# Sampled dilated attention moved out of a block of its own and woven into the compression; later modulation moved into the prompt attention

## The chip, the cores and the metric

The kernel runs on one core of one Trainium2 chip. The metric is device time in microseconds (us) of one execution. A core has five engines with queues of their own: TensorE (PE; its weight loads are shown as PEld), VectorE (DVE), ScalarE (ACT), GpSimd (POOL) and SyncE (SP, which here only issues transfers). They work in parallel and wait for one another on semaphores. Transfers are issued from the queues of SP, ACT and POOL and run on 16 DMA engines.

## The reference

One layer of a hybrid decoder, for a prompt of 512 tokens and for 8 sampled sequences of 4 tokens each (32 sampled tokens), with the same weights. Cut to what the change touches:

```
mod = silu(c) @ w_ada + b_ada                      # six groups of 1024: shift, scale, gate of mixer and of FFN
sh_m, sc_m, g_m, sh_f, sc_f, g_f = split(mod, 6)

# compression (branch A): rows of the key and value cache, paged, 4096 past tokens per sampled sequence
kc = compress_rows(kvc_full[:, 0], w1, pe, w2)     # conv of length 32, stride 16; gelu; @ w2
vc = compress_rows(kvc_full[:, 1], ...)

# dilated attention (branch C): 3 groups of 4 heads, (window, dilation) = (128,1), (512,4), (2048,16)
krow = n_prefix + q0 + arange(qb)[:, None] - offs[None, :]      # 129 rows of the cache for each query
s = einsum('bqhd,bhqkd->bhqk', q, kvg[:, 0]) * dk**-0.5 - bias
p, lse = masked_softmax(s, krow >= 0)
o = einsum('bhqk,bhqkd->bqhd', p, kvg[:, 1])
o_c = einsum('gbth,gbthd->bthd', softmax(lses), outs)           # the 3 groups merged
```

The first two of the six modulation groups are needed at once; the other four only after the mixer.

## The kernel before

The program is a chain of blocks. In each, every engine runs its own list of instructions in the order in which the code writes them, and the next block starts when all engines have ended theirs. Around the change the blocks are, in order:

1. `project_and_mix` (L1209): projection and the recurrent mixer. Several generators are merged on each engine by `weave` (L292): each yields a number, its place, and the generator with the lowest place writes its instructions next. The order is thus fixed when the program is built.
2. `sample_dilated` (L2433): the dilated attention of the 32 sampled tokens. One partition is one (head, sequence, token), 128 in all. For each of the three groups and for keys, then values, 129 rows of 64 numbers per partition are loaded into one of three buffers (`kv0` to `kv2`, 4.2 MB each), DVE multiplies a whole buffer by the query (L2569) and reduces it (L2570), ACT takes the exponential (L2523), and DVE multiplies the values by the weights (L2577) and reduces (L2578). Keys are loaded from SP's queue and values from POOL's (L2477 to L2485). In groups 1 and 2 the rows lie apart, so a transfer is made of pieces of 256 bytes; 16 large transfers make a buffer, each to 8 partitions. ACT's queue loads the four later modulation groups (`w_ada`, 16 MB in 8 transfers, L2518), PE multiplies them (L239, `modulation_step`), turns them (L246), and DVE adds the bias (L253). At its end SP issues 81 small transfers that write the new rows of the caches (`new_cache_rows`, L514).
3. `compress` (L1243): 36 units of work w, (sequence s, part c): 9 sequences (8 sampled, then the prompt) by 4 (keys and values of two heads). POOL gathers the pages of one whole sequence with 8 indirect transfers of 0.5 MB (L1307) into one of two buffers of four parts. For each unit PE transposes (L1337, `turn`), DVE splits each result into a high and a low part (L274, L279, `keep`), PE makes 48 matmuls (L1355, `hidden`), ACT applies gelu (L1389), PE projects (L1366, L1370), DVE copies the result. `turn(w + 1)` stands before `hidden(w)`.
4. `prompt_attention` (L1744): 48 units, 32 of kind A (8 heads, 4 query blocks; block qt sees qt + 1 blocks of keys) and 16 of kind C. PE: scores, transposes, values; DVE: bias and maximum; ACT: exponential, evacuation; POOL: scaling. SP loads the inputs, waits for them, and issues four large copies of the old caches to the outputs (`shift_caches`, L549, 47 MB).
5. `sample_nsa` and the rest, which the change leaves alone.

A `Chain` (L82) makes an engine wait for each of its own instructions before the next.

## Time and profile before

| | us |
|---|---|
| median of 3 runs | 2797.47 (2796.63 to 2809.92) |
| the profiled execution | 2810.91 |
| its span, first to last instruction | 2809.1 |
| PE busy | 2036.8 (73%) |
| DVE busy | 1357.4 (48%) |
| ACT busy | 442.3 (16%) |
| POOL busy | 310.0 (11%) |
| mean granted TensorE clock | 0.832 |

A span is cut into blocks by the first instruction of each. Busy times of engines overlap. The granted clock is a share of 2.4 GHz: 0.5 stands for 1.2 GHz, 1.0 for 2.4 GHz, and a value between says that a stretch held both. The DMA share is the mean busy share of the 16 DMA engines; since the packets of several queues overlap on an engine it can read a little over 1. A duration on SPq is how long SP was held by issuing the transfer, not how long the data took.

### The profile page before, as it was taken

How to read it: one execution, taken by the hardware profiler on the slowest of the kernel's cores; microseconds unless marked ns; L12 is line 12 of the kernel's file. 1: busy time of each engine (PE TensorE's matmuls, PEld its weight loads, DVE VectorE, ACT ScalarE, POOL GpSimd, SP SyncE). 2: the span in 40 equal slices, each digit the busy share in tenths (PEclk: the TensorE clock that was granted, in tenths of full speed). 3: DMA queues.
4: the chain of work that ended last, by engine and by line, in shares of the span. 5: the costliest groups of instructions: out<-in, count | busy, mean ns of one | idle time of the engine just before them, and what ended most of it. 6: DMA issues, size and time to landing. Idle time of an engine off the chain costs nothing. (4 is left out here: it accounts for less than half of the span.)

```text
span 2809.1 us, 38178 instructions
## 1 busy us (share of the span) xinstructions
PE 2036.8 (73%) x16050; PEld 1729.2 (62%) x16050; DVE 1357.4 (48%) x2126; ACT 442.3 (16%) x976; POOL 310.0 (11%) x350
## 2 busy tenths in 40 slices
PE   4986889789921002999959988127777976999995
PEld 2985778788910002899956566013435856999994
DVE  2135666665305533666605665454572346444444
ACT  1242333222200000000004454001111000000000
POOL 0000000000021212122003454004120000000000
PEclk7997999999965555999955898558878997999997
DMA  7434313122466863333139900127245103233220
GB/s 233 126 103 121 84 44 81 47 71 79 122 217 168 163 127 115 117 128 127 37 128 326 313 33 1 36 64 269 95 147 214 48 1 87 87 91 89 80 66 32
DMA packets 291913, 317.20 MB, mean 113 GB/s; under 512 B 92573, under 2 KB 246934, under 8 KB 287135
## 3 DMA queue, kind: packets, MB, share of 16 engines
q1 hardware_dynamic: 263998, 215.82, 26.2%
q0 software_dynamic: 24320, 79.94, 9.1%
q10 hardware_dynamic: 3424, 19.01, 2.1%
q8 instruction: 128, 2.10, 0.3%
q14 instruction: 43, 0.34, 0.0%
HBM read 287.10 MB, written 79.71 MB: 131 GB/s over the span
## 5 line engine op out<-in xcount | busy, mean ns | idle before, releaser
L307 PE MATMUL inp_acc<-hh,inp_wh 128*128 128x272 f32 (+1 forms) x1072 | 342.9, 320 | 32.6 <-DVE inp_wl L279 18.6
L307 PE MATMUL inp_acc<-hh,inp_wl 128*128 128x272 f32 (+1 forms) x1072 | 316.6, 295 | 0.0
L307 PE MATMUL inp_acc<-hl,inp_wh 128*128 128x272 f32 (+1 forms) x1072 | 316.2, 295 | 0.0
L307 PEld LDWEIGHTS inp_acc<-hh,inp_wh 128*128 128x128 f32 (+1 forms) x1072 | 207.9, 194 | 55.0 <-issue 27.7
L279 DVE TENSOR_TENSOR inp_wl<-inp_w,inp_wh 128x1024 fp32r<-128x1024 f32 (+1 forms) x67 | 81.2, 1213 | 268.4 <-ACT inp_wh L459 267.9
L307 PEld LDWEIGHTS inp_acc<-hl,inp_wh 128*128 128x128 f32 (+1 forms) x1072 | 208.5, 195 | 3.5 <-issue 3.1
L307 PEld LDWEIGHTS inp_acc<-hh,inp_wl 128*128 128x128 f32 (+1 forms) x1072 | 207.7, 194 | 0.5
L288 PE MATMUL ffn_acc<-ffn_hh,ffn_wh 128*128 128x272 f32 x704 | 147.3, 291 | 36.4 <-DVE ffn_wl L279 36.4
L1355 PE MATMUL cmp_pH<-cmp_RTh,cmp_w1h 128*128 128x256 f32 (+1 forms) x576 | 171.1, 297 | 2.7 <-issue 2.7
L1355 PE MATMUL cmp_pH<-cmp_RTh,cmp_w1l 128*128 128x256 f32 (+1 forms) x576 | 167.7, 291 | 3.0 <-issue 3.0
L1355 PE MATMUL cmp_pH<-cmp_RTl,cmp_w1h 128*128 128x256 f32 (+1 forms) x576 | 168.1, 292 | 2.0 <-issue 2.0
L1896 POOL TENSOR_SCALAR pat_s<-pat_s,pat_st 128x31 f32<-128x31 f32 (+2 forms) x144 | 127.3, 902 | 287.2 <-DVE pat_st L1924 238.8
L288 PE MATMUL ffn_acc<-ffn_hl,ffn_wh 128*128 128x272 f32 x704 | 146.6, 290 | 0.0
L288 PE MATMUL ffn_acc<-ffn_hh,ffn_wl 128*128 128x272 f32 x704 | 145.1, 287 | 0.0
L239 PE MATMUL sdi_acc<-sdi_w,cT 128*32 128x512 f32 x128 | 26.7, 979 | 153.2 <-DMA sdi_w<-in_w_ada_dram 153.2
L288 PEld LDWEIGHTS ffn_acc<-ffn_hh,ffn_wh 128*128 128x128 f32 x704 | 110.9, 190 | 36.8 <-DVE ffn_wl L279 36.8
L1355 PEld LDWEIGHTS cmp_pH<-cmp_RTl,cmp_w1h 128*128 128x128 f32 x576 | 118.2, 205 | 3.4 <-issue 3.4
L1355 PEld LDWEIGHTS cmp_pH<-cmp_RTh,cmp_w1h 128*128 128x128 f32 x576 | 117.6, 204 | 3.5 <-issue 3.1
L1355 PEld LDWEIGHTS cmp_pH<-cmp_RTh,cmp_w1l 128*128 128x128 f32 x576 | 117.5, 204 | 2.2 <-issue 2.2
L288 PEld LDWEIGHTS ffn_acc<-ffn_hl,ffn_wh 128*128 128x128 f32 x704 | 111.8, 190 | 0.0
L239 PEld LDWEIGHTS sdi_acc<-sdi_w,cT 128*32 128x32 f32 x128 | 4.6, 152 | 174.0 <-DMA sdi_w<-in_w_ada_dram 163.8
L288 PEld LDWEIGHTS ffn_acc<-ffn_hh,ffn_wl 128*128 128x128 f32 x704 | 111.5, 190 | 0.0
(443 smaller groups left out, 4109.1 us busy)
## 6 DMA issues: line engine op xcount, KB each, us to landing
inp_w<-in_w_in_dram SPq DMA_DIRECT2D x66, 512.0 KB, 4.3
out_dram<-in_cache_dil_dram SPq DMA_DIRECT2D x1, 32704.0 KB, 152.7
ffn_w<-in_w_ffn_dram SPq DMA_DIRECT2D x60, 512.0 KB, 4.0
sdi_w<-in_w_ada_dram ACTq DMA_DIRECT2D x8, 2048.0 KB
PT<-inp_o SPq DMA_DIRECT2D x58, 272.0 KB
sdi_kv<-in_cache_dil_dram POOLq DMA_DIRECT2D x36, 256.0 KB, 12.2
sdi_kv<-in_cache_dil_dram SPq DMA_DIRECT2D x36, 256.0 KB
ada_wada<-in_w_ada_dram SPq DMA_DIRECT2D x8, 1024.0 KB, 9.3
```

Of the source, the lines that this page charges most:

```text
L239: i = pe.matmul(out[32 * j:32 * j + 32, :], cT[:, k, :], w[:, 512 * j:512 * j + 512], start=(k == 0), stop=(k == KD - 1))
L279: return eng.tensor_tensor(lo, x, hi.bitcast(F32), ALU.subtract)
L288: i = pe.matmul(out[:, h, 0:HN], l, r[:, h * HN:(h + 1) * HN], start=(first and n == 0), stop=(last and n == 2))
L307: i = pe.matmul(out, l, r, start=(first and n == 0), stop=(last and n == 2))
L1355: i = pe.matmul(pH[:, w % 2, 0:nw], l, r, start=(q == 0 and n == 0), stop=(q == 15 and n == 2))
L1896: pool.tensor_scalar(s[:, u % 3, b, 0:n], s[:, u % 3, b, 0:n], st[:, u % 4, 2, b:b + 1], None, ALU.mult).then_inc(sd, 1)
```

## The change

`sample_dilated` is gone as a block. Its attention becomes the class `Dilated` (L1482 of the changed kernel), the compression becomes `Compression` (L1243), and `compress_and_dilate` (L1639) weaves the two in one block. The three buffers of 129 rows become three of 43 rows, so there are 18 loads ("pieces") instead of 6, all from SP's queue. The high part in the compression is written by ACT instead of DVE. The gathers go into a ring of six units instead of two sequences; the prompt's unit is read from `TM` by POOL's queue. The loads and matmuls of the later modulation are put between the units of the prompt attention, and `shift_caches` is issued from ACT's queue there. The wait for the new rows moves to the end of the program.

```
+class Compression:
+    NR = 6
+        self.R = lambda w: first[:, w % 6] if w % 6 < 4 else second[:, w % 6 - 4]
+    def pool(self, pool):
+        for w, (s, c) in enumerate(self.work):
+            if w >= self.NR:
+                pool.wait_ge(self.turned, self.read(w - self.NR))
+            elif w == 4:
+                pool.wait_ge(self.wfree, 3)
+            if s < DB:
+                for h in range(2):
+                    pool.indirect_dma_start(...).then_inc(self.got[w % self.NR], 16)
+    def tensor(self, pe):
+        for w in range(len(self.work)):
+            yield w
+            if w + 1 < len(self.work):
+                turn(w + 1)
+            yield w + 0.2
+            hidden(w)
+            yield w + 0.9
+            if w:
+                project(w - 1)
+    def scalar(self, act):
+                yield w + 0.1
+                high(w + 1)          # activation(RTh, pT, Copy), 4 per unit
+            yield w + 0.85           # then gelu of unit w
+    def vector(self, dve):
+                for j, x in enumerate(self.keep_at(w + 1)):
+                    yield w + 0.12 + 0.1 * j
+                    low(*x)          # split_low only
+            if w:
+                yield w + 0.95
+                result(w - 1)
+class Dilated:
+    NK = 129
+    PIECE = 43
+    NB = 3
+        self.order = keys[0] + keys[1] + vals[0] + keys[2] + vals[1] + vals[2]   # 3 pieces each
+    def transfers(self, i):
+        g, v, p = self.order[i]
+        return 16 if p < 2 else 32 if g == 0 else 20
+    def sync(self, sp):
+        self.load(sp, 0)
+        sp.wait_ge(self.qk, 2)
+        sp.dma_start(a["QC"], self.qt[:, :]).then_inc(self.qst, 16)
+        sp.wait_ge(self.qst, 16)
+        ...                          # 4 loads of the queries from QC
+        for i in range(1, len(self.order)):
+            if i >= self.NB:
+                sp.wait_ge(self.used, i - self.NB + 1)
+            self.load(sp, i)
+        new_cache_rows(sp, a, m["token_rows_out"])
+    def at(self, i, k):
+        return 0.5 + 1.8 * i + k
+    def vector(self, dve):
+        for i, (g, v, p) in enumerate(self.order):
+            yield self.at(i, 0)
+            if i == 0:
+                dve.wait_ge(self.loaded, 16 * 5)
+            dve.wait_ge(self.here[i % self.NB], self.arrived(i))
+            if v == 0:
+                c(dve.tensor_tensor(x, x, q..., ALU.mult))
+                yield self.at(i, 0.9)
+                c(dve.tensor_reduce(s[:, g, r], x, AX, ALU.add))
+                dve.sem_inc(self.used, 1)
+            ...                      # values alike
+        yield 50
+        dve.wait_ge(self.ft, 1)      # PE's last transpose; then 4 copies to ocT
 def prompt_attention(nc, a, m):
+    mod_at = [3 + 2 * l for l in range(KD)] + [24 + 2 * l for l in range(KD)]
+    turn_at = [mod_at[KD - 1] + 3, mod_at[2 * KD - 1] + 3]
-                sp.wait_ge(loaded, NLOAD)
-                shift_caches(sp, a, m["copied"])
+                for l in range(2 * KD):
+                    if l >= 4:
+                        sp.wait_ge(mstep, l - 3)
+                    sp.dma_start(wada[:, l % 4, :], a["w_ada"][...]).then_inc(wl[l % 4], 16)   # 1 MB
+                    if i in mod_at:                       # PE
+                        pe.wait_ge(wl[l % 4], 16 * (l // 4 + 1))
+                        modulation_step(pe, pM[:, :], m["cT"], wada[:, l % 4, :], l % KD).then_inc(mstep, 1)
+                    if i in turn_at:                      # PE
+                        pe.wait_ge(mevac, n + 1)
+                        modulation_turn(pe, pM[:, :], mm[:, n], m["ident"]).then_inc(mturned, 1)
                 act.wait_ge(loaded, NLOAD)
+                shift_caches(act, a, m["copied"])
-            sample_dilated(nc, a, m)
-NSA = [compress, prompt_attention, sample_nsa]
+NSA = [compress_and_dilate, prompt_attention, sample_nsa]
```

How the order moves on DVE, in the compression at the units around the first value pieces. Before, in the compression, the two halves of a split stood in a row, with nothing of the dilated branch:

```order
L274 CAST cmp_RTh<-cmp_pT 128x4x128
L279 TENSOR_TENSOR cmp_RTl<-cmp_pT,cmp_RTh 128x4x128
L274 CAST cmp_RTh<-cmp_pT 128x4x128
L279 TENSOR_TENSOR cmp_RTl<-cmp_pT,cmp_RTh 128x4x128
L274 CAST cmp_RTh<-cmp_pT 128x4x128
L279 TENSOR_TENSOR cmp_RTl<-cmp_pT,cmp_RTh 128x4x128
```

And the changed kernel, same engine (sdi_kv is a piece of 43 rows, cmp_RTl the low part that PE waits for, sdi_o the reduced values):

```order
L279 TENSOR_TENSOR cmp_RTl<-cmp_pT,cmp_RTh 128x4x128 x2
L1615 TENSOR_TENSOR sdi_kv<-sdi_kv,sdi_s 128x2752
L279 TENSOR_TENSOR cmp_RTl<-cmp_pT,cmp_RTh 128x4x128 x2
L1464 COPY vc<-cmp_pK 128x64
L1464 COPY vc<-cmp_pK 127x64
L279 TENSOR_TENSOR cmp_RTl<-cmp_pT,cmp_RTh 128x4x128
L1617 TENSOR_REDUCE sdi_o<-sdi_kv 128x64
L279 TENSOR_TENSOR cmp_RTl<-cmp_pT,cmp_RTh 128x4x128 x3
```

The casts have left DVE, and one instruction of a piece stands between the low parts of nearly every unit; the multiplication waits for the piece's transfers, and the low parts behind it wait with it.

On SP, the stretch from the last large loads to the new rows. Before:

```order
L2477 DMA sdi_kv<-TM 32x64
L2485 DMA sdi_kv<-in_cache_dil_dram 8x128x64 x4
L2477 DMA sdi_kv<-TM 32x64
L2485 DMA sdi_kv<-in_cache_dil_dram 8x128x64 x4
L519 DMA out_dram<-TM 512x4x64 x3
L525 DMA out_dram<-TM 128x4x64 x2
```

In the changed kernel:

```order
L1540 DMA sdi_kv<-in_cache_dil_dram 8x43x64 x32
L1529 DMA sdi_kv<-TM 32x64
L1540 DMA sdi_kv<-in_cache_dil_dram 8x42x64 x4
L1529 DMA sdi_kv<-TM 32x64
L1540 DMA sdi_kv<-in_cache_dil_dram 8x42x64 x4
L1529 DMA sdi_kv<-TM 32x64
L1540 DMA sdi_kv<-in_cache_dil_dram 8x42x64 x4
L1529 DMA sdi_kv<-TM 32x64
L1540 DMA sdi_kv<-in_cache_dil_dram 8x42x64 x4
L519 DMA out_dram<-TM 512x4x64 x3
```

The new rows keep their place behind the last load, but that load now waits for DVE's work on an earlier piece, late in the compression, and the loads that POOL issued stand on SP as well.

On PE, the prompt attention from its third unit on (pat_pS scores, pat_pX transposes, pat_pO values). Before:

```order
L1823 MATMUL pat_pS<-pat_kA,pat_qA 128x128 x2
L1835 MATMUL pat_pX<-ident,pat_s 31x128
L1835 MATMUL pat_pX<-ident,pat_s 128x128 x2
L1823 MATMUL pat_pS<-kcT,pat_qA 128x31
L1823 MATMUL pat_pS<-pat_kA,pat_qA 128x128 x2
```

In the changed kernel:

```order
L2051 MATMUL pat_pS<-pat_kA,pat_qA 128x128 x2
L2063 MATMUL pat_pX<-ident,pat_s 31x128
L2063 MATMUL pat_pX<-ident,pat_s 128x128 x2
L239 MATMUL pat_pM<-pat_wada,cT 32x512 x4
L2051 MATMUL pat_pS<-kcT,pat_qA 128x31
L2051 MATMUL pat_pS<-pat_kA,pat_qA 128x128 x2
```

One modulation step of four matmuls stands ahead of every second unit's scores, sixteen times in all.

## Rows read from the trace of the kernel before

**Rows 1.** Timeline: first SP issue of each block; start us, us, engine, line.

```profile
787.96 0.37 SPq L2492 DMA_DIRECT2D sdi_qf<-PT  x1
...
1087.98 0.37 SPq L1286 DMA_DIRECT2D cmp_pt<-in_page_lanes_dram  x1
...
1445.88 1.31 SPq L1798 DMA_DIRECT2D pat_qA<-PT  x2
...
1757.46 1.28 SPq L1992 DMA_DIRECT2D sco_qd<-PT  x2
```

**Rows 2.** Windows: span, busy us (count) of PE, PEld, DVE, ACT, POOL, clock, DMA share, GB/s.

```profile
1137.00:1400.00 263.00, 254.07 (x2075) 243.29 (x2073) 170.23 (x288) 16.18 (x33) 45.09 (x48) 0.99 0.29 99
...
1476.00:1545.00 69.00, 63.61 (x218) 43.74 (x219) 35.65 (x152) 27.21 (x122) 23.18 (x39) 0.50 1.02 332
1545.00:1757.00 212.00, 188.88 (x971) 128.77 (x970) 124.72 (x393) 95.47 (x328) 104.16 (x105) 0.88 0.36 115
```

**Rows 3.** Tile sdi_kv: DVE's passes over a whole buffer; duration ns min/median/max.

```profile
L2569 DVE TENSOR_TENSOR sdi_kv<-sdi_kv,sdi_q x3: 8758/8759/8760, 860.0 to 1025.3; 128x8256 f32<-128x8256 f32 x3
L2570 DVE TENSOR_REDUCE sdi_s<-sdi_kv x3: 8753/8753/8754, 868.8 to 1034.1; 128x129 f32<-128x8256 f32 x3
...
L2578 DVE TENSOR_REDUCE sdi_o<-sdi_kv x3: 13918/14032/14036, 887.7 to 1053.0; 128x64 f32<-128x8256 f32 x3
```

**Rows 4.** Groups by line: the split in the compression, DVE; busy us, mean ns.

```profile
L279 DVE TENSOR_TENSOR cmp_RTl<-cmp_pT,cmp_RTh 128x512 fp32r<-128x512 f32 (+1 forms) x136 | 90.8, 668 | 4.7
L274 DVE CAST cmp_RTh<-cmp_pT 128x512 fp32r<-128x512 f32 (+1 forms) x136 | 89.7, 660 | 19.8 <-PE cmp_pT L1337 19.7
```

**Rows 5.** Source line 467: ACT copying 128x512 out of PSUM, ns min/median/max.

```profile
L467 ACT ACTIVATE inp_tok<-inp_tb x18: 575/599/601, 174.5 to 407.1; 128x512 f32<-128x512 f32 x18
```

**Rows 6.** Timeline: PE at the compression's start, then ACT's gelu of three units.

```profile
1121.31 5.24 PE L1337 MATMUL cmp_pT<-ident,cmp_R 128*128 128x128 f32 x24 [6.57 <-DMA cmp_R<-in_cache_nsa_cmp_dram,idx]
...
1130.73 0.56 PE L1355 MATMUL cmp_pH<-cmp_RTh,cmp_w1h 128*128 128x256 f32 x1
...
1145.25 0.47 ACT L1389 ACTIVATE cmp_hid<-cmp_pH,cmp_hc 128x255 f32<-128x255 f32 x1 [5.63 <-PE cmp_pH L1355]
1153.44 0.47 ACT L1389 ACTIVATE cmp_hid<-cmp_pH,cmp_hc 128x255 f32<-128x255 f32 x1 [7.72 <-PE cmp_pH L1355]
...
1399.78 0.47 ACT L1389 ACTIVATE cmp_hid<-cmp_pH,cmp_hc 128x255 f32<-128x255 f32 x1 [6.61 <-PE cmp_pH L1355]
```

**Rows 7.** Windows, columns as rows 2: SP alone loading, SP and POOL loading, gathers.

```profile
860.00:880.00 20.00, 0.00 (x0) 0.00 (x0) 19.19 (x5) 0.50 (x2) 1.67 (x3) 0.50 0.52 112
...
920.00:940.00 20.00, 0.00 (x0) 0.00 (x0) 2.27 (x1) 0.00 (x0) 2.13 (x2) 0.50 0.90 123
...
1120.00:1130.00 10.00, 5.93 (x29) 5.44 (x29) 5.53 (x9) 0.00 (x0) 4.59 (x5) 0.67 1.03 413
```

**Rows 8.** Tile sdi_kv, SP's issues of group 0: ns min/median/max.

```profile
L2481 SPq DMA_DIRECT2D sdi_kv<-in_cache_dil_dram x16: 629/666/3230, 789.0 to 817.9; - x16
```

**Rows 9.** Timeline of SP: four loads among bulk transfers; the new rows, first and last.

```profile
877.36 33.49 SPq L2485 DMA_DIRECT2D sdi_kv<-in_cache_dil_dram  x4
...
1020.40 6.69 SPq L519 DMA_DIRECT2D out_dram<-TM  x3
...
1082.67 3.86 SPq L540 DMA_DIRECT2D out_dram<-TM  x6
```

**Rows 10.** Waits of PE from 1137 to 1400: us in total, times, longest.

```profile
PE cmp_pH L1355 <- issue: 7.7, 11, 1.1
```

**Rows 11.** Timeline: PE's modulation steps (8 records each); SP issuing the cache copies.

```profile
810.10 1.92 PE L239 MATMUL sdi_acc<-sdi_w,cT 128*32 128x512 f32 x16 [0.75 <-DMA sdi_w<-in_w_ada_dram]
...
904.00 3.64 PE L239 MATMUL sdi_acc<-sdi_w,cT 128*32 128x512 f32 x16 [7.39 <-DMA sdi_w<-in_w_ada_dram]
...
1471.66 0.64 SPq L556 DMA_DIRECT2D out_dram<-in_cache_nsa_win_dram  x1
1472.35 1.88 SPq L556 DMA_DIRECT2D out_dram<-in_cache_dil_dram  x3
```

More of the change, by code:

```diff
@@ new lines, in keep_at, with high @@
+    def keep_at(self, w):
+        s, c = self.work[w]
+        for k in range(self.mark[w], self.read(w)):
+            h, kq = (k - self.mark[w]) // 2, (k - self.mark[w]) % 2
+            yield (k, (slice(None), w % 2, slice(kq * 4, kq * 4 + 4), slice(h * P, h * P + self.rows(s))),
+                   self.pT[:, k % 4, :].rearrange("p (j c) -> p j c", j=4)[:, :, 0:self.rows(s)])
+    def scalar(self, act):
+        nc = self.nc
+        def high(w):
+            if w >= 2:
+                act.wait_ge(self.hd, w - 1)
+            for k, at, x in self.keep_at(w):
+                act.wait_ge(self.turned, k + 1)
+                nc.scalar.activation(self.RTh[at], x, ACT.Copy).then_inc(self.high, 1)
+        yield -0.9
+        act.wait_ge(self.wfree, 2)
+        high(0)
+        for w, (s, c) in enumerate(self.work):
+            if w + 1 < len(self.work):
+                yield w + 0.1
+                high(w + 1)
+            yield w + 0.85
+            act.wait_ge(self.hd, w + 1)
+            if w >= 2:
+                act.wait_ge(self.od, w - 1)
+            if w == 0:
+                act.wait_ge(self.hck, 1)
+            nc.scalar.activation(self.hid[:, w % 2, 0:self.nwin(s)], self.pH[:, w % 2, 0:self.nwin(s)], ACT.Gelu_apprx_tanh,
+                                 bias=self.hc[:, c // 2:c // 2 + 1]).then_inc(self.act, 1)
@@ L1300, in _ @@
[L1300 to L1310 removed]
+                cmp.pool(pool)
@@ L1312, in _ @@
             @block.tensor
             def _(pe):
-                pe.wait_ge(loaded, 80)
-                pe.transpose(pK[:, 0, 0:32], per[:, :], m["ident"][0:32, 0:32]).then_inc(pet, 1)
-                pe.wait_ge(pek, 1)
-                for v in range(2):
-                    for c in range(16):
-                        i = pe.matmul(pH[:, 0, v:v + 1], w1[:, v, c, :], peT[:, v * 16 + c:v * 16 + c + 1], start=(c == 0), stop=(c == 15))
-                i.then_inc(hcd, 1)
-                pe.wait_ge(hck, 1)
@@ L1342, in hidden @@
-                def hidden(w):
-                    s, c = work[w]
-                    pe.wait_ge(tkept, tmark[w] + 2 * nhalf(s))
-                    if w >= 2:
-                        pe.wait_ge(act_, w - 1)
-                    nw = nwin(s) + 1
-                    if w == 0:
-                        pe.wait_ge(wfree, 3)
-                    for q in range(16):
-                        lo, hi = w1l[:, c // 2, q, :], w1h[:, c // 2, q, :]
-                        x = slice(q // 8, q // 8 + nw)
-                        xh, xl = RTh[:, w % 2, q % 8, x], RTl[:, w % 2, q % 8, x]
-                        for n, (l, r) in enumerate(((hi, xh), (hi, xl), (lo, xh))):
-                            i = pe.matmul(pH[:, w % 2, 0:nw], l, r, start=(q == 0 and n == 0), stop=(q == 15 and n == 2))
-                    i.then_inc(hd, 1)
@@ L1444, in _ @@
-                keep(0)
-                for w in range(len(work)):
-                    if w + 1 < len(work):
-                        keep(w + 1)
-                    if w:
-                        result(w - 1)
-                result(len(work) - 1)
+                weave(cmp.vector(dve), dil.vector(dve))
 def layer_norm_t(nc, a, m, tag, xin, out_tokens=None, gain="ln1"):
```

588 lines of the change are left out of this document (295 added, 293 removed).

## The prediction, made blind

> **What bounds the kernel now.** I read the timeline of SP first, for where one block ends and the next begins [rows 1]. The dilated branch holds the core from 787.96 to 1087.98 us, 300.0 us; the compression from there to 1445.88, 357.9 us; the prompt attention to 1757.46, 311.6 us. Then the windows, for who is busy in each. In the steady compression PE is busy 254 of 263 us at the full clock, DVE 170, ACT 16, and the DMA share is 0.29 [rows 2]: PE sets the end, and DVE, ACT and the DMA engines have room. Which room, the tiles tell. A pass of DVE over a whole buffer takes 8.76 us (the weighting of the values has the same shape) and the reduction of the values 14.03 [rows 3], so three groups cost 3 x (8.76 + 8.75 + 8.76 + 14.03) = 120.9 us of DVE. In the attention PE is busy 63.6 of 69 us at half clock up to 1545, and 188.9 of 212 us at a mean of 0.88 afterwards [rows 2]: PE bounds it too, closely at first and less so later.
>
> **Part 1, the block removed.** All of 300.0 us goes: DVE, DMA waits, and the new rows that SP issues last [rows 1]. This is the one large gain. What it held must now fit beside the compression (dilated attention, new rows) and beside the attention (modulation).
>
> **Part 2, DVE and ACT in the compression.** A unit takes PE 1153.44 - 1145.25 = 8.2 us in steady state, and (1399.78 - 1145.25)/30 = 8.5 us on average over the 30 units from w = 1 to 31 [rows 6]; I use 8.5. The four casts of a unit (0.66 us each) leave DVE, which keeps four subtractions (0.67 us) [rows 4], 2.7 us, and about 0.4 us of results. A piece is a third of a buffer: 2.9 + 2.9 us for keys, 2.9 + 4.7 us for values [rows 3], one piece every 1.8 units, so 3.2 to 4.2 us per unit. DVE then has 6.3 to 7.3 us of work in 8.5. ACT gets four copies of 128x512 out of PSUM at 0.6 us [rows 5], with gelu 2.9 us per unit. Neither becomes the bound. A low part can now be late by one DVE instruction, 4.7 us at most; `turn(w + 1)` precedes the 48 matmuls of unit w, most of its 8.2 us, so the four subtractions still end within the unit. I cost this at nothing; if the cover is gone it is 1 to 2 us in a few units.
>
> **Part 3, the transfers of the pieces, where I see the new bound.** A piece is 128 x 43 x 256 bytes = 1.41 MB. In groups 1 and 2 (12 of 18 pieces) it moves in 256-byte parts. SP alone moved these at 112 GB/s with a DMA share of 0.52; SP and POOL together at 123 GB/s with a share of 0.90 [rows 7]. So a second queue brought nothing, and a piece takes 11.5 to 12.6 us; I take 12. Its 16 issues (0.67 us each [rows 8], 10.7 us) lie within that; the last piece of three has 20, I take 15 us, and 32 in group 0, 21 us. Gathers ran at 413 GB/s [rows 7]: 1.05 MB per unit is 2.5 us, 4.6 us in 1.8 units. Do the two add up or overlap? The nearest row says that added traffic is paid: four loads of 1 MB in all held SP for 33.5 us while bulk transfers ran [rows 9], 9 us by the rate alone. I take the sum, 17 us for a piece with gathers beside it, against 1.8 x 8.5 = 15.3 us in which PE uses one up. The bounds are 12.5 (full overlap) and 20.
>
> The Trainium skill ("DMA: Bandwidth & Descriptors", section "Why a DMA increments its semaphore by 16 and not by 1") states that a transfer is spread over the largest number up to 16 that divides its slowest dimension, on SP's queue over the lowest-numbered engines. These transfers go to 8 partitions, so by that rule all pieces would sit on the same 8 engines, which agrees with the share of 0.52; gathers on all 16 would queue behind them there, and the sum (17) would hold rather than the overlap (12.5).
>
> Now SP's chain, in us from the block's start. The queries come back from `QC` near 37, when SP can go on to piece 1. Pieces 1 and 2 (11 and 21) end at 69. Pieces 3, 4, 5: 17 + 17 + 19, at 122. Pieces 6 to 8 (group 0's values, large parts): 12 + 12 + 21, at 167. Pieces 9 to 14: 106, at 273. Gathers, six units ahead, are over by then: 12 + 12 + 15, at 312. Behind it stand the 81 new rows, which took 1086.5 - 1020.4 = 66 us [rows 9]: SP ends at 378. PE's chain: the first hidden matmul came 42.7 us after the block's start, after a wait of 6.6 us for gathers of a whole sequence [rows 6]; two gathers are enough now, I take 39 (bounds 36 and 43). Piece i is needed at 39 + 8.5 x (0.5 + 1.8 i): 89 for piece 3, 120 for 5, 201 for 10, 257 for 14. By the chain above they land at about 88, 124, 203 and 275: PE loses some 17 us behind DVE's wait in all. Then 357.9 - 42.7 - 1 = 314 us of units as before, and 2 us for the last transpose and copies: 39 + 314 + 17 + 2 = 372. SP ends later, 378, plus the 1.5 us from its last issue to the next block as before: **379.5 us against 357.9, +21.6**. Bounds: with full overlap SP is held back only by the buffers (piece 14 consumed near 267, + 15 + 66 = 348) and PE ends at 355, so -1; with 20 us for each of the nine pieces beside gathers, +49. Instruction fetches stopped PE 11 times for 7.7 us [rows 10] at a DMA share of 0.29; with more traffic I expect more, within the 6 us by which PE trails SP.
>
> **Part 4, the attention.** The input loads are unchanged. The four cache copies, 0.64 + 1.88 us of issue on SP [rows 11], now stand ahead of ACT's first scaling, on which PE waits: +2.5. A modulation step takes 3.64/2 = 1.8 us at half clock and 1.92/2 = 0.96 at full [rows 11]. Of the 16, six fall into the half-clock stretch: 6 x 1.8 + 10 x 0.96 = 20.5 us. PE has hardly a gap for them. The two turns, with waits for ACT and DVE, 3. Against that, the step is dense, and after two in a row the clock rose even in idle surroundings, while the attention's first 69 us ran at 0.50 [rows 2]. If the steps lift it there for a third of the time, about 10 us come back (bounds 0 and 30, half of 63.6). Sum 2.5 + 20.5 + 3 - 10 = **+16**, between -4 and +26. The w_ada loads (1 MB per two units, 10 us or so) share the engines with 47 MB of copies at 332 GB/s [rows 2]; four buffers of lead cover that.
>
> **Sum.** 2809.1 - 300.0 + 21.6 + 16 = 2546.7 us of span, 2548.5 with the 1.8 us around it. The profiled execution (2810.9) is 13.4 us above the median of three, one of which is as long. Taking that off: **2535 us**.
>
> **Rivals.**
> A, the transfers overlap: part 3 gives -1 instead of +21.6 and part 4 +5, as the clock rises more: 2535 - 23 - 11 = 2501. For it: a share of 0.52 leaves half the engine time free. Against: rows 9.
> B, the transfers add up more badly: 20 us per piece (+27) and no help from the clock (+10): 2572. For it: the 33.5 us. Against: those bulk loads were far denser than the gathers.
> C, PE loses its instructions: if each of the 36 units had a stop of 2.4 us instead of 7.7 us in all, 86 - 8 = 78 more, less the 6 of slack: 2607. Against: the present stops are 1.1 us at most [rows 10], though at gather bursts.
> D, slower than before: every piece is starved as in the 33.5 us row. 1 MB in 33.5 us makes 45 us per piece, 17 of them 765, with 37 before and 66 + 1.5 after: 869.5, +512 instead of +22, so 3025. It decides from (357.9 + 284 - 104.5)/17 = 31.6 us per piece. It needs bulk traffic all the time, while gathers alone need 2.5 us of 8.5.
> E, the weaving brings nothing beyond moving the wait (PE stops for each piece and its clock halves): a unit then costs up to double at half clock; at a third of the 31 large units, 10 x 8 = 80, 2615. The share of PE's waiting would have to be far above the 17 us worked out.
>
> **Chances.** Forecast 0.44, A 0.26, B 0.18, C 0.04, E 0.04, D 0.03, 0.01 for a time below A. Predicted 2535. The range runs from 2490, a little below A, to 2600, B with its execution in the upper of the two levels seen; it leaves out C, D, E and the tails. A measurement of this kernel can tell some 0.5% (14 us) from no change. Faster 0.95, same 0.02, slower 0.03.
>
> **What would show it.** Block lengths from SP's first issues: the compression 360 to 400 us; under 360 says A. Its end: last issue of the new rows, not PE's last transpose; the other way round says that SP is not the bound. DVE's wait for sdi_kv: near zero for pieces 0 to 4, then 2 to 5 us at heavy pieces. SP held about 17 us per heavy piece. DVE busy near 75% there. In the attention 16 steps, half of them near 1.8 us and a clock above 0.5 before the 384-column scores. Wrong would be: DVE or ACT as the last releaser of PE's transposes without a piece behind it, a wait of PE for w_ada, or a compression above 410 us.

## The result, and the profile of the changed kernel

The changed kernel takes 2641.27 us (median of 4 runs, 2634.51 to 2647.57), the kernel before 2803.27 us beside it (2796.63 to 2809.92). The ratio is 0.942, 95% interval 0.939 to 0.945: 5.8% faster. The prediction was 2535 us, range 2490 to 2600. Its direction was right; it was 106 us too fast, and the time lies outside its range.

Its profiled execution took 2641.51 us, with a span of 2639.7. The timeline of SP gives the block starts again (start, us, engine, line), to be laid beside [rows 1]:

```profile
790.46 0.33 SPq L1285 DMA_DIRECT2D cmp_pt<-in_page_lanes_dram  x1
...
1189.45 1.36 SPq L2022 DMA_DIRECT2D pat_qA<-PT  x2
...
1589.69 1.25 SPq L2242 DMA_DIRECT2D sco_qd<-PT  x2
```

| us | before | forecast | after |
|---|---|---|---|
| up to the compression (dilated block included before) | 1088.0 | 788.0 | 790.5 |
| compression | 357.9 | 379.5 | 399.0 |
| prompt attention | 311.6 | 327.6 | 400.2 |
| the rest | 1051.6 | 1051.6 | 1050.0 |

So the block that went gave 297.5 us where 300 were forecast (with the blocks ahead of it, which the change leaves alone, ending 2.5 us later), the compression took 19.5 us more than forecast, and the attention 72.6 us more. The attention is the larger miss, so I read it first. Windows of the changed kernel (span, busy us and count of PE, PEld, DVE, ACT, POOL, clock, DMA share, GB/s), a stretch of the compression and two of the attention:

```profile
833.00:1110.00 277.00, 243.13 (x1930) 233.27 (x1930) 190.02 (x195) 84.40 (x157) 61.86 (x52) 0.94 0.65 178
...
1230.00:1340.00 110.00, 63.11 (x237) 36.58 (x238) 30.00 (x127) 22.13 (x105) 20.92 (x36) 0.53 1.01 341
1340.00:1500.00 160.00, 129.38 (x695) 79.47 (x694) 77.59 (x259) 60.54 (x212) 64.02 (x69) 0.85 0.38 131
```

PE is busy 63 of 110 us where [rows 2] had 63.6 of 69, and its clock stays at 0.53. The DMA engines are full (1.01, 341 GB/s). The waits of the attention's stretch (us in total, times, longest) and the timeline of PE's modulation steps name what it stands behind:

```profile
PE pat_pM L239 <- DMA pat_wada<-in_w_ada_dram: 67.3, 5, 19.9
```

```profile
1252.13 1.93 PE L239 MATMUL pat_pM<-pat_wada,cT 128*32 128x512 f32 x8
...
1270.33 1.94 PE L239 MATMUL pat_pM<-pat_wada,cT 128*32 128x512 f32 x8 [7.39 <-DMA pat_wada<-in_w_ada_dram]
...
1302.08 1.94 PE L239 MATMUL pat_pM<-pat_wada,cT 128*32 128x512 f32 x8 [19.52 <-DMA pat_wada<-in_w_ada_dram]
...
1333.38 1.94 PE L239 MATMUL pat_pM<-pat_wada,cT 128*32 128x512 f32 x8 [19.87 <-DMA pat_wada<-in_w_ada_dram]
...
1364.60 1.94 PE L239 MATMUL pat_pM<-pat_wada,cT 128*32 128x512 f32 x8 [19.78 <-DMA pat_wada<-in_w_ada_dram]
```

The first four loads were issued ahead of the copies. The first three are in time, the fourth comes 7.4 us late (the row at 1270.33); then a megabyte comes every 31 us (1302.08, 1333.38, 1364.60), while two units of PE's work take 10 to 12. The page's section on transfers (KB each, median us from issue to landing; packets and MB of ACT's queue):

```profile
out_dram<-in_cache_dil_dram ACTq DMA_DIRECT2D x1, 32704.0 KB, 161.8
pat_wada<-in_w_ada_dram SPq DMA_DIRECT2D x16, 1024.0 KB, 27.8
...
q10 hardware_dynamic: 2080, 50.23, 5.5%
```

In the compression the waits of its stretch, then SP's timeline and DVE's last work in the block:

```profile
DVE sdi_kv L1605 <- DMA sdi_kv<-in_cache_dil_dram: 52.1, 6, 11.7
PE cmp_pT L1332 <- DVE cmp_RTl L279: 33.8, 8, 7.7
...
DVE sdi_kv L1615 <- DMA sdi_kv<-in_cache_dil_dram: 13.6, 6, 6.3
```

```profile
860.01 37.76 SPq L1540 DMA_DIRECT2D sdi_kv<-in_cache_dil_dram  x32
...
1121.57 5.63 SPq L519 DMA_DIRECT2D out_dram<-TM  x3
...
1183.65 3.86 SPq L540 DMA_DIRECT2D out_dram<-TM  x6
```

```profile
1174.86 0.77 DVE L1636 COPY ocT<-cmp_pK 64x32 f32<-64x32 f32 x4 [0.58 <-PE cmp_pK L1576]
```

DVE waited 65.7 us for pieces, and PE 33.8 us behind it, where the forecast had PE lose 17. SP ends last, as forecast: 12 us after DVE's last copy (1187.5 against 1175.6) where the forecast had 6, and both later than forecast.

### The profile page after: what moved, and what is told of

Read it like the earlier page. It is cut to its first block and busy times, and to the rows that moved or that the text cites. A ratio compares the mean times of both kernels' runs of the same rounds, so it can differ in the third digit from the quotient of the medians.

```text
span 2639.7 us, 38466 instructions
## 1 busy us (share of the span) xinstructions
PE 2032.3 (77%) x16050; PEld 1728.5 (65%) x16050; DVE 1271.1 (48%) x2016; ACT 520.9 (20%) x1119; POOL 270.6 (10%) x282
## 3 DMA queue, kind: packets, MB, share of 16 engines
q10 hardware_dynamic: 2080, 50.23, 5.5%
## 5 line engine op out<-in xcount | busy, mean ns | idle before, releaser
L307 PE MATMUL inp_acc<-hh,inp_wh 128*128 128x272 f32 (+1 forms) x1072 | 342.7, 320 | 32.7 <-DVE inp_wl L279 18.5
L1306 POOL DMA_INDIRECT cmp_R<-in_cache_nsa_cmp_dram,idx x44 | 51.1, 1162 | 860.7 <-DVEq L1433 748.4
L2113 ACT ACTIVATE pat_s<-pat_s,pat_st 128x31 f32<-128x31 f32 (+2 forms) x144 | 70.2, 488 | 228.6 <-DVE pat_st L2155 173.5
## 6 DMA issues: line engine op xcount, KB each, us to landing
pat_wada<-in_w_ada_dram SPq DMA_DIRECT2D x16, 1024.0 KB, 27.8
```

The lines of the kernel that those rows point to most:

```text
L307: i = pe.matmul(out, l, r, start=(first and n == 0), stop=(last and n == 2))
L1306: pool.indirect_dma_start(out=self.R(w)[:, h, :], out_offset=None, in_=src, in_offset=bass.IndirectOffsetOnAxis(ap=self.m["idx"][:, c, 2 * ...
L2113: nc.scalar.activation(s[:, i % 3, b, 0:n], s[:, i % 3, b, 0:n], ACT.Exp, bias=st[:, i % 4, 0, b:b + 1], accum_out=st[:, i % 4, 1, b:b + 1 ...
```

## Experiments

The theories at the start. **W**: the `w_ada` loads are starved by the cache copies. **P**: the sixteen steps cost that much by themselves. For the compression, **G**: pieces and gathers add up on the transfers; against it, that DVE's and ACT's new work delays PE. The chip varies between sessions: the kernel before took 2810 to 2811 us (medians) beside runs 1 to 8 and 2779 to 2780 beside 9 to 12, where the blocks behind the attention take 13 us less. I therefore compare by ratio to the kernel before, and by blocks. No trace of the kernel before was taken beside runs 9 to 12, so where the other 18 of its 31 us went isn't known; the ratios of these runs are the surer measure. The blocks are those of one profiled execution each. Where a run leaves transfers out or splits them, the counts that are waited for change with it and aren't shown.

| run | compression | attention | rest | ratio |
|---|---|---|---|---|
| changed kernel | 399.0 | 400.2 | 1050.0 | 0.942 (0.939 to 0.945) |
| 1 copies late | 397.5 | 316.9 | 1111.6 | 0.933 (0.930 to 0.936) |
| 2 no loads | 394.4 | 336.6 | 1050.1 | 0.917 (0.913 to 0.920) |
| 3 finer cut | 398.6 | 407.2 | 1051.6 | 0.940 (0.935 to 0.944) |
| 4 rows moved | 383.5 | 439.8 | 1053.4 | 0.949 (0.946 to 0.953) |
| 5 packets 19 KB | 394.8 | 373.2 | 1050.6 | 0.927 (0.922 to 0.932) |
| 6 packets 5 KB | 398.7 | 369.2 | 1047.7 | 0.927 (0.923 to 0.931) |
| 7 no gathers | 347.1 | 410.6 | 1051.4 | 0.923 (0.918 to 0.929) |
| 8 no pieces | 341.5 | 406.6 | 1050.1 | 0.920 (0.914 to 0.926) |
| 9 paced | 398.4 | 328.7 | 1037.1 | 0.918 (0.915 to 0.921) |
| 10 paced, early piece | 397.1 | 327.1 | 1037.1 | 0.916 (0.912 to 0.919) |
| 11 all | 381.5 | 315.8 | 1036.5 | 0.913 (0.911 to 0.915) |
| 12 half rows | 393.3 | 436.0 | 1037.5 | 0.956 (0.953 to 0.960) |

### 1. The copies issued late

```
                 for l in range(2 * KD):
                     ...                       # wait, load of w_ada
+                sp.wait_ge(mstep, 2 * KD)
+                shift_caches(sp, a, m["copied"])
-                shift_caches(act, a, m["copied"])
```

> The changed kernel, with the four cache copies (47 MB) issued by SP after the last modulation step instead of by ACT at the start of the prompt attention. Theory W (the 1 MB loads of w_ada are starved by the copies, PE stands behind each, and its clock stays low): no wait of PE for w_ada (67 us in the changed kernel), and the attention falls from 400 us to 311.6 + 16 - 2.5 = 325 us. The copies then run for some 160 us, most of it in the next block: the rest grows by 0 to 30 us. In all 2641 - 75 + (0 to 30) = 2566 to 2596 us. Rival P (the sixteen steps of matmuls cost this much by themselves, by their own time at half clock and by what they push back): the attention stays above 380 us, all in all 2620 to 2641. Rival C (whoever runs beside the copies pays the same price as the modulation did): the attention falls by 75 us and the rest grows by as much, 2641.

The attention fell to 316.9 us, below what W expected, with no wait of PE for `w_ada`; a load landed 4.9 us after its issue (median) instead of 27.8. Theory P is out. But 62 of the 83 us came back in the next block, more than W allowed and near to rival C. The waits from the next block on, and the windows of the attention's first 80 us and of the next block's:

```profile
DVE sna_QD L2308 <- DMA sco_tri<-in_c_tri_dram: 98.7, 1, 98.7
```

```profile
1223.00:1303.00 80.00, 77.98 (x335) 44.82 (x334) 41.41 (x167) 30.13 (x135) 28.12 (x45) 0.66 0.31 104
...
1503.00:1583.00 80.00, 0.00 (x0) 0.00 (x0) 0.00 (x0) 0.00 (x0) 0.00 (x0) 0.50 0.87 276
```

The next block begins with loads too, and they were late in the same way: that wait was 35.7 us in the changed kernel. Here too the bulk copy delayed who loaded beside it. In the attention the steps, now on time, cost 316.9 - 311.6 = 5.3 us net. The clock is at 0.66 in the window from 40 to 120 us after the block's start, where the same stretch of the kernel before (1486 to 1566 us) has 0.61; how much of the steps' price that gave back, the run doesn't tell.

### 2. The loads left out

```
+                    if l < 4:
                         sp.dma_start(wada[:, l % 4, :], ...)
-                        pe.wait_ge(wl[l % 4], 16 * (l // 4 + 1))
+                        pe.wait_ge(wl[l % 4], 16)
```

> The changed kernel without the w_ada loads 5 to 16 (left out; the steps multiply the first four buffers again), with the cache copies where they were. It tells the price of the steps beside the copies from that of the late loads. Theory W: PE waits for nothing here once the first four loads are in, the attention takes 325 to 335 us, in all about 2570. Rival P: the steps themselves cost, the attention stays near 400, 2640. Rival I (the copies slow PE in another way, through its instruction fetches): PE's idle time without a releaser is tens of us and the attention stays above 370 us.

336.6 us with the copies where they were and all sixteen steps on PE: W, 1.6 us above its range. Rival I is out, since PE has no wait without a releaser in the block. One of the first four loads still came 8.5 us late. What is left over before is 336.6 - 311.6 = 25.0 = 8.5 + 2.7 (ACT's issues) + 13.8 for steps and turns, net of what the clock gave; the forecast had 20.5 + 3 - 10 = 13.5.

### 3. The copies cut finer

```
-... ("dil1", 512, 8, 4), ("dil2", 2048, 8, 28)):
+... ("dil1", 512, 8, 16), ("dil2", 2048, 8, 112)):
```

> The changed kernel with the two largest cache copies cut four times finer (pieces of 4.7 KB instead of 18.7 KB for the largest); bytes, queue and place as before. Theory T (a DMA engine takes a piece from each queue in turn, so a queue's share goes by the size of its pieces): w_ada's rows of 8 KB got 1 MB in 30 us, about 35 GB/s of 330; against pieces a quarter as large its share at least doubles, a load takes 8 to 15 us, and the attention falls to 330 to 350 us; in all 2570 to 2590. Rival B (the share doesn't hang on the pieces' size, the loads stand behind bytes already queued): a load stays at 30 us and the attention at 400, 2641. A cost of the finer pieces themselves would show as a longer time of the copies than 162 us.

PE waited 67.4 us for `w_ada`, and it is no evidence for rival B: ACT's queue held the same packets as before, so the finer cut never reached the queue: neighbouring pieces that lie behind one another had been joined again. The run tested nothing. It gave the number that the theory lacked: the four copies are 832 of the 2080 packets (1248 are left on this queue in run 1), 48.0 MB or 58 KB each on average. (That average counts 64 packets of 4 bytes, the semaphore's; the single records of the trace, under run 12, have 512 packets of 65,408 bytes, 192 of 65,024 and 64 of 31,744.)

```profile
q10 hardware_dynamic: 2080, 50.23, 5.4%
```

### 4. The new rows moved into the attention

```
         for i in range(1, len(self.order)): ...
-        new_cache_rows(sp, a, m["token_rows_out"])
 # attention, SP, behind each w_ada load from the 5th on:
+                    next(rows, None)          # 9 of the 81 stores
```

> The changed kernel with the 81 stores of new rows moved from SP's end of the compression to SP in the attention, 9 at a time behind the w_ada loads 5 to 13. Theory S (SP's tail sets the end of the compression): the block ends with PE and DVE, 399 - 12 = 387 us. Rival N (they delay something only on paper; PE's chain ends it as well and gains nothing): 397 to 399 us. The attention: the stores hold SP some 8 us per step, less than the 30 us that a load is late anyway; +0 to +15 us. In all 2641 - 12 + (0 to 15): 2629 to 2644 by S, 2641 to 2656 by N.

Half of theory S held: the compression fell to 383.5 us, by 15.5. The attention rose by 40, well beyond both. SP's timeline and PE's wait:

```profile
1218.89 142.73 SPq L524 DMA_DIRECT2D out_dram<-TM  x3
```

```profile
PE pat_pM L239 <- DMA pat_wada<-in_w_ada_dram: 109.1, 3, 79.4
```

The first stores have rows of 256 bytes, 2048 of them for half a megabyte, and held SP until the copies were nearly over; every `w_ada` load stood behind them.

### 5 and 6. Copies in smaller packets

From run 3's packet count comes **T**: a DMA engine takes a packet from each queue in turn. A load has 9 packets on each engine (twelve loads fewer in run 2 are 1728 packets fewer, 144 each, by 16 engines). A copy packet of 58 KB at 330/16 GB/s takes 2.8 us, and 9 such turns, with 3 us for the load itself, make the 28 us of a load.

```
-sp.dma_start(dst.rearrange("r (c n) -> r c n", c=cut), src...)
+sp.dma_start(dst.rearrange("r (c n) -> c r n", c=cut), src...)   # run 6: cut 4 times larger
```

> The changed kernel with the cache copies written with the piece index outermost, so that neighbouring pieces can't be joined again: 18.7 KB for the largest cache, at most 32.5 KB for the others. In the run with the finer cut the packets had stayed what they were (2080 on ACT's queue in both, 832 of them with 48 MB from the copies, 58 KB each), so it had tested nothing. Theory T (an engine takes one packet from each queue in turn): a w_ada load has 9 packets on each engine; at 330/16 = 20.6 GB/s a copy packet of 58 KB takes 2.8 us, so a load 9 x 2.8 + 3 = 28 us, as seen (27.8); with 18.7 KB it takes 9 x 0.9 + 3 = 11 us (17 behind the 32.5 KB ones). PE's wait for w_ada falls from 67 to 5 to 20 us, the attention from 400 to 335 to 350 us, in all 2575 to 2590. Rival B (the size doesn't matter, the loads stand behind bytes already queued): a load stays near 28 us, the attention at 400, 2641. The copies themselves: 162 us if the packet size costs nothing.

> As the run with packets of 19 KB, with each piece four times smaller: 4.7 KB and 8.1 KB. Theory T: a load takes 9 x 0.23 to 0.4 + 3 = 5 to 7 us, no wait of PE for w_ada but perhaps the first loads, the attention 328 us (336.6 in the run without the loads, less its one wait of 8.5 us), in all 2641 - 72 = 2569, plus what later blocks lose if the copies last beyond 162 us. Rival B: 2641. Rival Q (small packets make the copies so slow that they reach into the next block): copies over 300 us, and the next block's first loads late, as in the run with late copies, +20 to +60.

In both PE's wait for `w_ada` was gone, as T says, but the attention fell only to 373.2 and 369.2 us. Run 6's windows, landing time, and the timeline of ACT:

```profile
1266.00:1366.00 100.00, 96.41 (x418) 57.49 (x419) 51.75 (x203) 39.20 (x169) 38.03 (x57) 0.68 1.01 359
```

```profile
pat_wada<-in_w_ada_dram SPq DMA_DIRECT2D x16, 1024.0 KB, 9.8
```

```profile
1213.09 40.78 ACTq L556 DMA_DIRECT2D out_dram<-in_cache_dil_dram  x3
1253.92 1.91 ACT L2102 ACTIVATE pat_qA<-pat_qA 128x2048 f32<-128x2048 f32 x1 [83.46 <-issue]
```

With the engines as full as before (1.01, 359 GB/s) PE is busy 96 of 100 us. What remained is a new wait that I had not seen coming: issuing so many packets held ACT 41 us (44 in run 5), and PE's first scores stand behind ACT's scaling. Since ACT was held, fewer bytes were queued at once, so these two runs don't separate T from a rule of queued bytes; run 12 was made for that.

### 7 and 8. Gathers left out; pieces left out

```
+            if self.NR <= w < 4 * DB:         # run 7, POOL: no gathers for units 6 to 31
+                continue
```

```
-            if i >= self.NB:                  # run 8, SP: only the first three pieces
-                sp.wait_ge(self.used, i - self.NB + 1)
-            self.load(sp, i)
+            if i < self.NB:
+                self.load(sp, i)
```

> The changed kernel without the gathers of units 6 to 31 (left out; the units use the first six again). It tells what of a piece's time is the gathers'. In the changed kernel two heavy pieces hold SP for 37.8 us, 18.9 each, beside gathers. Theory G (pieces and gathers add up, 12 us alone): 12 to 13 us per heavy piece, SP is then held back by the buffers, so its time per piece follows DVE's use, 1.8 units or 15.3 us; DVE's wait for sdi_kv falls from 66 us to under 15, the compression ends with piece 18 used near 312 and the new rows behind it: 399 - 20 = 378 us or less. Rival E (the pieces are slow by themselves, by eight of the sixteen engines or by reads of 256 bytes): 17 to 19 us per piece as before, 395 to 399 us.

> The changed kernel without the loads of pieces 4 to 18 (left out; DVE computes on the first three again), gathers as they were, and the new rows issued at once. It prices DVE's and ACT's woven work alone. Theory G and the prediction (the weaving costs PE nothing, the transfers do): PE ends near 39 + 314 + 2 = 355 us after the block's start, the block takes 357 us against 399. Rival V (DVE's long instructions between the low parts delay PE's transposes even when all data is there): 365 to 385 us, PE's waits for the low part stay at 34 us. The new rows here lie at the compression's start beside the gathers; the attention after it stays at 400.

Run 8, then run 7: the window of the steady compression in each, and SP's two heavy pieces (32 issues) in run 7.

```profile
833.00:1110.00 277.00, 276.69 (x2225) 267.81 (x2224) 214.67 (x228) 91.66 (x177) 60.96 (x52) 0.95 0.39 119
```

```profile
833.00:1110.00 277.00, 276.69 (x2223) 267.82 (x2221) 214.93 (x228) 91.43 (x177) 2.71 (x4) 0.95 0.43 101
```

```profile
857.74 24.49 SPq L1542 DMA_DIRECT2D sdi_kv<-in_cache_dil_dram  x32
```

With all of DVE's and ACT's new work in place PE is busy 276.7 of 277 us: the weaving costs PE nothing, and rival V is out. The first two heavy pieces take 24.49/2 = 12.2 us each without gathers and 37.76/2 = 18.9 with them, so they add up, and the gathers beside a piece cost 6.7 us. Over all nine pieces beside gathers SP is held 120.9 us without them and 173.1 with them, 5.8 us a piece. With either left out the block takes 347 and 342 us, less than the 357.9 of before, which I had not expected. In the kernel before, nearly every fourth unit took 10.4 us where its neighbours took 7.9 or 8.2, at the end of each burst of eight gathers; the one that came behind the last burst took 8.2. Run 8 has 240.7 us from the gelu of unit 1 to that of unit 31, against the 254.5 of [rows 6], and run 7, without gathers, the same 240.7. Of these 13.8 us, 7.7 are the stops of [rows 10], which run 8 doesn't have. Whether the ring or the casts that went to ACT took them away, no run separates.

### 9 to 11. Paced copies, an earlier piece, the rows behind the copies

```
+    for name, w, heads, count, cut in (("win", 512, 4, 2, 16), ("dil0", 128, 8, 1, 1),
+                                       ("dil1", 512, 8, 4, 16), ("dil2", 2048, 8, 16, 32)):
+        ...                                   # count transfers of 2.1 MB, each in cut pieces a row
 # attention, SP, behind the w_ada load l (run 9):
+                    for _ in range(4 if l == 3 else 6 if l == 11 else 3 if l == 15 else 1 if l > 3 else 0):
+                        y, x = next(parts)
+                        sp.dma_start(y, x).then_inc(m["copied"], 16)
-                shift_caches(act, a, m["copied"])
 # compression, SP, ahead of the wait for the queries (runs 10 and 11):
+        self.load(sp, 1)
 # attention, SP (run 11): the 81 stores behind the loads l = 11 to 15
+                    for _ in range(2 if l == 11 else 4 if l == 15 else 1 if l > 11 else 0):
+                        next(rows)
```

> The changed kernel with the cache copies cut into 23 transfers of 2.1 MB (packets of 16.3 KB, 8.1 KB and 31.7 KB), each issued by SP right behind a w_ada load: 4 after the 4th, one after each of the 5th to 11th and 13th to 15th, 6 after the 12th, 3 after the last; none from ACT. Theory T (a load loses by what copy packets are queued beside it, and only while they are): a part takes 6.5 us at 330 GB/s, a step comes every 12 us, so a load of 3 to 10 us is always in time; ACT is not held (42.9 and 25.6 us for one issue in the runs with small packets). PE waits for no w_ada, the attention takes 317 us (as with the copies late) to 325 us (336.6 without the loads, less its one wait of 8.5 and 2.7 of ACT's issues), the rest stays at 1050: 2641 - 80 = 2561, 2553 to 2572. Rival H (SP is held by the parts as ACT was, and the loads behind them are late): PE waits again, 20 to 60 us. Rival C (the copies only push their price elsewhere, as the late ones did by 62 us in the next block): the rest grows, 2590 to 2620.

> As the run with paced copies, and SP loads the second piece before it waits for the queries' way through memory. SP's chain starts 11.4 us earlier with it: the new rows end, and with them the compression, at 399 - 8 to -11 = 388 to 391 us if SP's chain is what sets the block's end and the pieces' times (theory S); DVE's wait for pieces, 66 us, falls by about as much. In all 10 us below the run with paced copies. Rival N (the pieces' time under the gathers stays the pace, and the buffers hold SP back, so the lead is lost by the 4th piece): within 3 us of it.

> As the run with paced copies and the early piece, and the 81 stores of new rows taken from SP's end of the compression to SP in the attention, after the 12th w_ada load and later, when most copies are done (beside all copies they had held SP for 142.7 us). Theory S: the compression loses its tail and ends with PE's work, 383.5 us as in the run that moved them, less what the early piece gives (PE's end 0 to 10 us earlier): 374 to 384 us; the attention grows by 0 to 5 us. In all 2561 - 15 - (0 to 10) = 2536 to 2548. Rival H (the stores hold SP beside the last copies again and w_ada loads 13 to 16 come late): PE's waits for w_ada 10 to 60 us, 2560 to 2600.

Run 9, windows of the attention:

```profile
1220.00:1340.00 120.00, 113.13 (x495) 68.33 (x495) 64.30 (x248) 48.13 (x201) 46.58 (x66) 0.70 1.00 361
1340.00:1500.00 160.00, 141.21 (x747) 91.94 (x745) 93.95 (x295) 70.05 (x242) 74.83 (x74) 0.88 0.31 111
```

The same bytes, the engines as full, no wait for `w_ada` at all, ACT not held, and PE busy 113 of 120 us. The attention takes 328.7 us, 4 more than the upper end expected for it, and nothing comes back later (the rest is 1037.1 us, and 1037.5 in run 12 with the copies as they were). The ratio says the same as the blocks: 0.942 - 0.918 is 67 us. Three things differ from the changed kernel, though: the pacing, packets of 8 to 32 KB instead of 65, and the copies on SP's own queue instead of ACT's. No run separates them. Run 10 comes out at rival N's time, but not by its mechanism. The compression gained 1.3 us. The queries' way through memory took longer behind the early piece: their four loads begin 41.8 us after the block's start instead of 34.3 in run 9, DVE's wait for them rose from 7.4 to 12.5 us, and the lead was used up there, before any buffer could hold SP. Run 11: the tail is gone from the compression (381.5), and in its profiled execution the attention is 13 us shorter than in run 9, although the first stores held SP 42 us beside six parts of the copies:

```profile
1286.05 42.37 SPq L519 DMA_DIRECT2D out_dram<-TM  x3
```

No step was late there, since the loads were four ahead. In that execution the clock is higher: PE's first scores come 30.4 us after the block's start in runs 9 and 11 alike, but in the windows that follow the clock is at 0.77 and 0.93 in run 11 where run 9 has 0.70 and 0.88. This is no gain of the version, as far as the times tell: the profiled execution (2520.85 us, mean clock 0.877) was the fastest of five by 12.7 us, the others took 2533.5 to 2538.3 at 0.869 to 0.872, and the medians of runs 10 and 11 lie 14.0 us apart, no more than the compression's 15.6. Run 11 is the fastest version, 0.913 of before against 0.942 for the changed kernel.

### 12. The loads in twice the packets

```
-    sp.dma_start(wada[:, l % 4, :], a["w_ada"][..., t:t + ADA_W])
+    for c in range(2):                        # 4 KB rows
+        sp.dma_start(wada[:, l % 4, 1024 * c:1024 * c + 1024], a["w_ada"][..., t + 1024 * c:t + 1024 * c + 1024])
```

> The changed kernel, copies untouched (from ACT, 58 KB packets), with each w_ada load of 1 MB made of two transfers with rows of 4 KB instead of one with rows of 8 KB: the same bytes in the same buffers in twice the packets. The runs with smaller copy packets had also changed how many bytes were queued at once, since ACT was held while issuing them; this one changes only the loads. Theory T (an engine takes one packet from each queue in turn): 18 packets per engine and load, 18 x 2.8 us = 50 us per load plus its own 3, so the modulation steps beside the copies stand 50 to 55 us apart instead of 31 (steps 5, 6, 7 of the changed kernel), PE's longest wait for w_ada is 38 to 44 us instead of 19.9; the copies end after some 160 us anyway, so only two or three such waits: 90 to 110 us in all instead of 67, and the attention takes 420 to 440 us, in all 2665 to 2680. Rival B (the share goes by bytes, or by what stands queued): steps 31 us apart, longest wait 20, 2641.

```profile
1267.21 1.94 PE L239 MATMUL pat_pM<-pat_wada,cT 128*32 128x512 f32 x8 [25.12 <-DMA pat_wada<-in_w_ada_dram]
...
1328.29 1.94 PE L239 MATMUL pat_pM<-pat_wada,cT 128*32 128x512 f32 x8 [50.27 <-DMA pat_wada<-in_w_ada_dram]
```

The two steps stand 61.1 us apart instead of 31: twice the packets, twice the time for the same megabyte, 3.4 to 3.5 us a packet in both (61.1/18, 31.2/9). PE waited 102.6 us in all. The attention takes 436.0 us. Bytes, and what stands queued, are the same as in the changed kernel, so rival B is out, and T's turn is longer than the 2.8 us that I had put.

The trace of the changed kernel holds every packet with its queue, size and time, and these records show the turns themselves. From 1275 to 1365 us, 416 packets of SP's queue start (368 of 8192 bytes and 48 of the semaphore's 4) and 417 of ACT's: one for one. A copy's packet has 65,408 bytes and takes 3.12 us (median), a load's 0.31. Eight such turns and a ninth packet of the copy make 30.6 of the 31.2 us. In run 12 a load's packet takes 0.16 us and a copy's 3.17, and sixteen turns with two more packets of the copy make 59.6 of the 61.1.

## Why the prediction failed, point by point

**Part 1** held: 297.5 of the 300 us went. **The bound** held for the kernel before, but in the changed kernel PE waits in both blocks: behind the pieces in the compression, whose end SP sets, and for `w_ada` in the attention up to 1365 us.

**Part 2** (DVE and ACT cost nothing) held, as run 8 shows. It was even better: PE's own part of the block is 340 us (run 8, to DVE's last copy) and not the 355 of "314 us of units as before", since the slow units at the gathers' bursts are gone, 13.8 us. The trace of before had them in [rows 6]: 8.2 us for a plain unit, 8.5 on average. I took the average for PE's own pace.

**Part 3** had the right mechanism (the two kinds of traffic add up) and the right order at the end (SP last), and mis-sized terms. The heavy piece was put at 12 + 4.6 = 17 us; the first two measured 18.9, where the 12 was right (12.2, run 7) and the gathers' part was 6.7. The nine pieces beside gathers were put at 159 us, 117 of them their own; they took 173.1, of which 120.9 are their own (run 7) and 52.2 the gathers'. SP's chain was thus at 286 us after piece 14, where I had 273. Pieces 15 to 17 were put at 39 us by their own rate; they took 44.8, and 44.8 without gathers as well, so here their own time was put too low. It wasn't the buffers that held SP. These are all its waits from 790 to 1190 us, and none is for a buffer:

```profile
SPq L101 <- PEq L101: 1.4, 3, 0.6
SPq L1645 <- PEq L1645: 0.2, 1, 0.2
```

The buffer of piece 16, for one, was free at 1075.0 us, and SP came to it at 1091.9. 13 and 6 us make the 19 by which the block was missed, through the 66 us of new rows behind. PE lost 287.4 - 240.7 = 46.7 us in the large units (gelu of unit 1 to that of 31, here and in run 8) instead of 17, since its own pace was faster than I took it and the pieces came later than I took them; SP's tail hid this, and in run 4, without the tail, the block takes 383.5 us. Two readings were wrong besides. Piece 10 is needed at 196 us by the formula given (39 + 8.5 x 18.5), not at 201; the loss of 17 hung on piece 14 and doesn't change. And [rows 10] show stops in which PE waited for nothing that the profile shows, 7.7 us; that they were instruction fetches is not shown.

**Part 4** holds the step that failed: "The w_ada loads (1 MB per two units, 10 us or so) share the engines with 47 MB of copies at 332 GB/s; four buffers of lead cover that." They cover it for three loads, and the fourth is 7.4 us late. Behind them a load takes 31 us against 10 to 12 us of use, and no lead covers a lasting deficit. I compared the loads' bytes with the rate, 16 MB beside 47 MB, in 190 us of transfers, and this does fit, as run 9 shows; but a queue doesn't get its share by bytes. The row to size it by was in the argument already: four loads, 1 MB in all, that held SP 33.5 us among bulk transfers [rows 9]. I used it in part 3, where the traffic beside the pieces was light, and not in part 4, where a megabyte among bulk transfers was the very case; it took 31 us here. Of the 88.6 us, 67.3 are the waits and 2.7 ACT's issues, as forecast; 18.6 are left for the steps, where run 2 has 13.8 and the forecast 13.5. Most of the missing 5 us is the clock: PE stood still for 47 of 110 us, its clock stayed at 0.53 up to 1340 us, and ten steps ran at half clock, at 1.93 us each, instead of six. The steps alone took 25.7 us here and 22.1 in run 2. "A wait of PE for w_ada" stood in the list of what would be wrong, with no rival and no chance of its own.

The Trainium skill ("DMA: Bandwidth & Descriptors", section "Queues, rings and completion order") states that each DMA engine goes round the queues that have work and changes at packet boundaries. By that rule the share goes by the sizes of packets, and the traces agree (31 and 61 us for 9 and 18 packets of a load, 416 packets against 417). The section's packet holds several descriptors, typically 9 to 17; what the trace counts as packets alternated one by one, each a single row of a load, and it is these that share the engines here. The same page's rule on how many engines a transfer uses was weighed in part 3; runs 7 and 8 show the sum that it allowed, but not which engines were used.

**The rivals.** E's time (2615) came nearest, by another cause: the clock in the steady compression stayed at 0.94. Of the two on either side of part 3, B was the better: 18.9 us a piece, 19.2 as the mean of all nine, lies between the forecast's 17 and its 20, and A, the overlap, is out by run 7 beside the changed kernel. C is out: of stops without a releaser, 7.7 us before, PE has none in this block now; from 833 to 1185 us all but 0.4 us of its waits are for a low part, 34.1 us. D was far off (18.9 us a piece against its 31.6).

**What stays open.** Which of pacing, smaller packets and the common queue did the work in run 9; which part of the change freed PE of its stops of before; whether spreading the pieces over more engines would shorten them (it was not tried); and what moves the attention between 400 and 411 us from one execution to the next, as the changed kernel and runs 3, 7 and 8 do with the same work in it.

## What to carry to other kernels

A load that has to arrive on time beside a bulk copy on another queue took, here, the number of its packets times the time of one packet of the copy, and half as large packets made it twice as slow; a lead of buffers only puts that off. What worked here was to cut the bulk copy into transfers of 2.1 MB (6.5 us each by the rate, an estimate) with packets of 8 to 32 KB, and to issue each behind a load that is needed, instead of all at once; the total traffic then fitted where the sum of bytes says it does. And a stretch of average pace that holds stops is not the engine's own pace: take the plain unit, and say where the rest goes.

## What the runs showed of the hardware that I had not expected

- A 1 MB load with rows of 8 KB took 31 us beside copies with packets of 65 KB, and 61 us with rows of 4 KB; 9.8 us (issue to landing) beside packets of 5 to 8 KB, at 359 GB/s in all.
- With both queues full, their packets started one for one: 416 against 417 in 90 us, although one kind is eight times as large.
- Transfers with rows of 256 bytes held SP for 142.7 us beside the copies (run 4).
- ACT was held 41 and 44 us by issuing three copies in thousands of small packets (runs 6 and 5), which it issued in 1.9 us when they had 65 KB packets.
- Pieces that lie behind one another in memory on both sides had been joined when they reached the queue: a cut of 4 and 28 or of 16 and 112 gave the same 2080 packets on the queue.
